# Handing 29 of the first 64 ada weight chunks from VectorE to TensorE in a two-block fp32 transformer kernel

## The chip, the cores and the metric

One NeuronCore of one Trainium2 chip runs the whole program. The metric is the device time of one launch in microseconds (us), as the median of several runs. The kernel before takes 3055.92 us (3 runs, 3054.85 to 3061.74).

## The reference, cut to what matters

Two transformer blocks in fp32 on a sequence of 256 rows with model width 2048. The change touches only the very first step of the first block, the modulation vector, and what it feeds:

```python
mod = (c @ w_ada[l] + b_ada[l])[:, None, :]      # c: 1 x 2048, w_ada: 2048 x 12288
shift1, scale1, gate1, shift2, scale2, gate2 = jnp.split(mod, 6, axis=-1)
h = rmsnorm(x, g_pre_mix[l]) * (1.0 + scale1) + shift1
proj = h @ w_in[l]                               # everything else of the block follows from proj
```

`c @ w_ada` is one row times a matrix of 96 MB. Its first third (scale1 and shift1, 4096 columns, 32 MB) has to be known before `h`, and so before the first real matmul can run. The other two thirds are computed later, beside other work, and are not touched.

## The kernel before, in words

Everything is kept transposed: features on the 128 partitions, the 256 rows of the sequence along the free dimension.

**The matmul jobs.** All large matmuls go through one helper, `job` (its matmuls are recorded at line L1494). Weights arrive in chunks of 128 x 1024 fp32 in a ring of four `raw` slots. ScalarE rounds a chunk to `w_hi` (L607 for the first four chunks, L630 later), VectorE makes the rest `w_lo` (L967 for the first four, L1005 later), and TensorE multiplies both with the operand `X`. TensorE takes its instructions strictly in the order of its program, and the jobs follow each other from `kv`, the first, to the end of the kernel.

**The opening stage.** Before the job `kv` can go on, the kernel computes scale1 and shift1. The 32 MB are cut into 64 chunks, each of 128 rows of `w_ada` (index k, 16 of them) by 1024 columns (`ADA_CB`), 512 KB. Sixteen chunks make a block; the four blocks are taken in the order `FIRST_BLOCKS = (2, 0, 3, 1)`: scale1 first half, shift1 first half, scale1 second half, shift1 second half. So chunk number `at` is block `at // 16`, row group `at % 16`.

SyncE's queue loads the chunks in order into 12 staging slots (`stage`, L484), with x (`x1`, 2 MB) after chunk 5, the constants after chunk 9, and the first four `raw` chunks of `w_in` behind chunks 34 and 38 and at the end. Chunk n waits until VectorE has used chunk n - 12 (`stage_used`). A load that waits holds back all that stand behind it in the queue.

VectorE (`first_block`) multiplies each chunk by the 128 values of c that belong to its rows and adds it to an accumulator of 128 x 1024, `first_acc`: L1079 for the first chunk of a block, L1081 for the other 15. Between chunks it does other small work, put there by hand: results of the block before, the normalised x (`unit_x`, L1148), the bounds, the second half of X.

TensorE (`first_ada`) then adds the accumulator over the partitions: 8 matmuls, each with 128 columns of `first_acc` as the stationary operand and a 128 x 2 tile of ones as the moving one. The trace records each such fp32 matmul as two weight loads and two matmuls. VectorE adds the bias (`first_result`, L1089), and so on to the coefficients of X.

TensorE's own order in this stage is: `norm_sum(sq1)` (16 fp32 matmuls of 128 x 256 that add up the squares of x), `first_ada(0)`, `first_ada(1)`, `first_ada(2)`, then the first two chunks of the job `kv`, `first_ada(3)`, and the rest of `kv`. ScalarE squares x before `norm_sum` (L649) and makes the reciprocal root from its sum behind it (L652, L653). The first halves of X are written by ScalarE (L688) and the second ones by VectorE (L1113).

Of the kernel before, what the change touches and what calls it, by code (L numbers as in the profile page):

```python
# [16 lines left out]
P = 128  # L17
# [22 lines left out]
ADA_CB = 1024  # L40
STAGES = 12
FIRST_BLOCKS = (2, 0, 3, 1)

PAR = {}
# [98 lines left out]
def two_block_kernel(nc, xT, params, cons, level_in, count_in, hot_in, rel_bias, pos, w_ada, w_in, w_attn, w_hgrn, w_out,  # L144
                     w_ffn_in, w_ffn_out, w_in2, pool_w, w_out2, w_up, w_down, out, stop_after=None):
    ctx = ExitStack()
    with ctx:
# [117 lines left out]
        def sem(name):  # L265
            return ctx.enter_context(nc.semaphore(name))
# [10 lines left out]
        ada_pair, ada_half, ada_split = sem("ada_pair"), sem("ada_half"), sem("ada_split")  # L277
        ada_mm, ada_out = sem("ada_mm"), sem("ada_out")
        staged = [sem(f"staged{n}") for n in range(STAGES)]
        stage_used, mod_ready = sem("stage_used"), sem("mod_ready")  # L280
        dve_chain = sem("dve_chain")
        act_chain = sem("act_chain")
        act_parted, sp_parted, pool_parted = sem("act_parted"), sem("sp_parted"), sem("pool_parted")
# [71 lines left out]
        def ahead(j, i, p, final):  # L355

            q = p + RING
            if q < j.n:
                return j, i, q
            if not final:  # L360
                return j, i + 1, q - j.n
            return (j.next, 0, q - j.n) if j.next is not None else None

        def half_slot(j, q):

# [98 lines left out]
        def P_(name, a=0, b=None):  # L464
            lo, hi = PAR[name]
            return par[:, lo + a:(hi if b is None else lo + b)]
# [6 lines left out]
        @block.sync  # L473
        def _(sp):
            sp.dma_start(par[:, :], params).then_inc(par_in, 16)
            ada_v = w_ada.rearrange("(k p) n -> p k n", p=P)

            def first_weights(q):
                sp.dma_start(raw[:, q, :, :], w_src(jobs[0], 0, q)).then_inc(landed[q], 16)
            for n in range(ADA_FIRST * DT):  # L480
                m, k, s = FIRST_BLOCKS[n // DT], n % DT, n % STAGES
                if n >= STAGES:
                    sp.wait_ge(stage_used, n - STAGES + 1)
                sp.dma_start(stage[s][:, :], ada_v[:, k, m * ADA_CB:(m + 1) * ADA_CB]).then_inc(staged[s], 16)  # L484
                if n == 5:
                    sp.dma_start(x1[:, :, :], xT.rearrange("(t p) s -> p t s", p=P)).then_inc(x_in, 16)
                if n == 9:
                    sp.dma_start(con[:, :], cons).then_inc(con_in, 16)
                if live and n in (2 * DT + 2, 2 * DT + 6):
                    first_weights(0 if n == 2 * DT + 2 else 1)  # L490
            for q in (2, 3) if live else ():
                first_weights(q)

            def load(j, i, k, src, flat_=False):

                s = slot_of(j, k)
                sp.wait_ge(raw_used, landing(j, i, k) - RING + 1)
                if not is_static(i):
                    sp.sem_inc(sp_parted, 1)
                dst = raw[:, s, :, :].rearrange("p k n -> p (k n)") if flat_ else raw[:, s, :, :]  # L500
                sp.dma_start(dst, src).then_inc(landed[s], 16)

            def job_turn(j, i, final):
                for p in range(j.n):
                    nxt = ahead(j, i, p, final)
                    if nxt:
                        load(j, i, j.at[p], w_src(*nxt))
                    for k, a in enumerate(j.ada):
                        if a == p:
                            load(j, i, j.ada_at(k), ada_v[:, k, ds((j.m0 + i) * ADA_CB, ADA_CB)], True)  # L510
            for j in live:
                all_turns(sp, j, job_turn)
# [435 lines left out]
        def _(dve):  # L948
# [119 lines left out]
            def first_block(n, between={}):  # L1068
                for k in range(DT):
                    at = n * DT + k  # L1070
                    s = at % STAGES
                    if k == 0 and n >= 2:
                        dve.wait_ge(ada_mm, n - 1)
                    if k >= 1:
                        dve.wait_ge(stage_used, at)
                    dve.wait_ge(staged[s], 16 * (at // STAGES + 1))
                    ck, acc = P_("c", k, k + 1), first_acc[:, n % 2, :]
                    if k == 0:
                        ins = nc.vector.tensor_scalar(acc, stage[s][:, :], ck, None, ALU.mult)  # L1079
                    else:  # L1080
                        ins = nc.vector.scalar_tensor_tensor(acc, stage[s][:, :], ck, acc, ALU.mult, ALU.add)  # L1081
                    ins.then_inc(stage_used, 1)
                    if k in between:
                        between[k]()

            def first_result(n):
                m = FIRST_BLOCKS[n]
                dve.wait_ge(ada_mm, n + 1)
                nc.vector.tensor_tensor(mod[:, m * 8:m * 8 + 8], pss[:, 3, 496:512:2], P_("b_ada", m * 8, m * 8 + 8), ALU.add  # L1089
                                        ).then_inc(ada_out, 1)  # L1090

            def first_scale(n):
                first_result(n)
                dve.wait_ge(ada_out, n + 1)
                t0 = 8 * (n // 2)
                here(nc.vector.scalar_tensor_tensor(coef[:, 0, t0:t0 + 8], mod[:, DT + t0:DT + t0 + 8], 1.0,
                                                    P_("g_pre_mix", t0, t0 + 8), ALU.add, ALU.mult))

            def first_shift(n):
                first_result(n)  # L1100
                dve.wait_ge(ada_out, n + 1)
                dve.sem_inc(mod_ready, 1)

            def first_full(q):
                for t in range(4 * q, 4 * q + 4):
                    ins = nc.vector.tensor_scalar(sq1[:, t, :], x1[:, t, :], coef[:, 0, t:t + 1], mod[:, t:t + 1],
                                                  ALU.mult, ALU.add)
                here(ins)

            def first_low(q):  # L1110
                t = slice(4 * q, 4 * q + 4)
                dve.wait_ge(nrm_hi, q + 1)
                nc.vector.tensor_tensor(X[:, t, S:2 * S], sq1[:, t, :], X[:, t, 0:S].bitcast(F32), ALU.subtract  # L1113
                                        ).then_inc(nrm_out, 1)
# [35 lines left out]
            def bounds():  # L1150
# [6 lines left out]
                here(nc.vector.tensor_scalar(cosq[:, :], cosk[:, :], HD1 ** -0.5, None, ALU.mult))  # L1157
                here(nc.vector.tensor_scalar(sinq[:, :], sink_[:, :], HD1 ** -0.5, None, ALU.mult))

            first_block(1, {4: lambda: first_scale(0), 6: unit_x, 10: bounds})  # L1160
            splits = (lambda: split_first(0), lambda: split_first(1)) if live else (lambda: None,) * 2
            first_block(2, {4: lambda: first_shift(1), 6: lambda: first_full(0), 7: lambda: first_low(0),
                            9: lambda: first_full(1), 10: lambda: first_low(1), 12: splits[0], 14: splits[1]})
            first_block(3, {4: lambda: first_scale(2)})
            if live:
                split_first(2)
# [325 lines left out]
        def _(pe):  # L1492
            def mm(out_, l, r_, start=True, stop=True):
                return nc.tensor.matmul(out_, l, r_, start=start, stop=stop)  # L1494
# [76 lines left out]
                        pe.wait_ge(nrm_out, 4 * k + c + 1)  # L1571
                return ready

            norm_sum(sq1)

            def first_ada(n):
                pe.wait_ge(stage_used, (n + 1) * DT)
                if n:
                    pe.wait_ge(ada_out, n)
                for t in range(8):  # L1580
                    ins = mm(pss[:, 3, 496 + 2 * t:498 + 2 * t], first_acc[:, n % 2, t * P:(t + 1) * P], ones[:, 0:2])
                ins.then_inc(ada_mm, 1)
            pe.wait_ge(ones_set, 2)
            for n in range(3):
                first_ada(n)
            pe.sem_inc(S1["pv"], 1)
            pe.sem_inc(SH["sb"], 1)
            pe.sem_inc(SH["o"], 1)
            if runs("kv"):
                pe.wait_ge(con_in, 16)  # L1590
                pe.wait_ge(ones_set, 3)

                def side(i, p):
                    if p == 1:
                        first_ada(3)
                job(J["kv"], lambda g: X, x_ready(), side)

                def side(i, p):
                    if is_first(i):
                        return  # L1600
                    if p == 0:

                        mm(pss[:, 0, 0:S], C_("rope_swap"), proj[:, KA, :]).then_inc(S1["swap"], 1)
                        for a in range(2):
                            ins = nc.tensor.transpose(pss[:, 2, a * P:(a + 1) * P], proj[:, VA, a * P:(a + 1) * P], C_("ident"))
                        ins.then_inc(S1["vt"], 1)
                    if p == 2:

                        pe.wait_ge(S1["kr"], 1)
                        for g in range(2):  # L1610
                            mm(pss[:, 1, g * S:(g + 1) * S], C_("kv_pick", g * P, (g + 1) * P), kr[:, :]).then_inc(S1["dup"], 1)
                job(J["qa"], lambda g: X, None, side)
# [235 lines left out]
```

## Time and profile before

| | |
|---|---|
| median of 3 runs | 3055.92 us |
| the profiled execution | 3053.75 us |
| its span | 3052.0 us |
| mean granted TensorE clock | 0.925 |
| TensorE matmul busy | 2674.7 us, 88% |
| VectorE busy | 1833.3 us, 60% |
| ScalarE busy | 1310.0 us, 43% |
| DMA | 550.85 MB, mean 180 GB/s |

Busy times are those of one profiled execution, and shares are shares of its span. The profiled execution is 2.17 us under the median of the runs. A granted clock of 1.00 is 2.4 GHz, 0.50 is 1.2 GHz. Rows are in us from the start of the span unless they say ns; "x16" is a count of recorded instructions, and what stands behind "<-" in a row of a tile is what is read. PEld is TensorE's weight load, PE its matmul, SPq SyncE's DMA queue, DVE VectorE, ACT ScalarE.

### The profile page before, as it was taken

Reading aid. Unit: us, or ns where it says so; the run is one execution under the profiler, and the core shown is the slowest. Engines: PE = TensorE matmul, PEld = TensorE weight load, DVE = VectorE, ACT = ScalarE, POOL = GpSimd, SP = SyncE. Lnnn points to the kernel's source line nnn. Section 1 sums busy time; section 2 is a strip of 40 time slices with the busy share of each in tenths; the row PEclk is TensorE's granted clock in tenths of the full one; section 3 lists DMA queues with packets and bytes.
Section 4 is the critical chain, followed back from the end, with each engine's and each line's share of the span. In section 5 each row is a group of like instructions: output and inputs, shape, how many; then the busy total and the mean of one; then the engine's idle time right before and its main releaser. Section 6 shows DMA issues by size and latency. Waiting matters only on the chain.

```text
span 3052.0 us, 40694 instructions
## 1 busy us (share of the span) xinstructions
PE 2674.7 (88%) x14562; PEld 2302.2 (75%) x14562; DVE 1833.3 (60%) x2057; ACT 1310.0 (43%) x1585; POOL 73.4 (2%) x56
## 2 busy tenths in 40 slices
PE   2598886666799769999979999799889999999998
PEld 1577776565687658888768887688778888888887
DVE  7766665666566655556655554644547766456664
ACT  1244443333443344444334444454445555445542
POOL 0000000000000000000000000001000000000000
PEclk7798887878899879999989999899899999999999
DMA  9767773222368726668756655365344566555664
GB/s 379 229 198 228 239 234 105 86 78 83 103 188 274 250 80 186 186 185 261 257 185 182 187 188 166 102 180 154 110 145 154 177 191 193 189 179 184 192 190 141
DMA packets 473580, 550.85 MB, mean 180 GB/s; under 512 B 16728, under 2 KB 446816, under 8 KB 473488
## 3 DMA queue, kind: packets, MB, share of 16 engines
q1 hardware_dynamic: 471408, 542.10, 56.0%
q0 software_dynamic: 2080, 7.52, 0.8%
q8 instruction: 59, 0.97, 0.1%
q14 instruction: 33, 0.27, 0.0%
HBM read 547.44 MB, written 2.11 MB: 180 GB/s over the span
## 4 chain that ended last, share of the span: by engine, by line
PE 66%; DVE 12%; issue 10%; DMA 5%; ACT 5%; POOL 1%; SPq 1%; ACTq 0%; DVEq 0%; POOLq 0%
PE psg L1494 60%; PE pss L1494 5%; ACT w_hi L630 2%; DMA raw<-in_w_ffn_out 2%; DVE first_acc L1081 2%; DMA raw<-in_w_out 2%; DVE w_lo L1005 2%; DVE s_ab L1298 1%; DVE ada_acc L986 1%; DVE masked L1295 1%; POOL ada_acc L529 1%; DMA raw<-in_w_ffn_in 1%; DVE Pq L1281 1%; DVE sq L1042 0%; DVE X L1047 0%
## 5 line engine op out<-in xcount | busy, mean ns | idle before, releaser
L1494 PE MATMUL psg<-X,w_hi 128*128 128x512 f32 x4768 | 1721.0, 406 | 35.2 <-issue 22.1
L1005 DVE TENSOR_TENSOR w_lo<-raw,w_hi 128x1024 fp32r<-128x1024 f32 x832 | 1024.7, 1244 | 914.3 <-ACT w_hi L630 905.7
L1494 PE MATMUL psg<-X,w_lo 128*128 128x256 f32 x4768 | 1331.4, 284 | 0.0
L630 ACT ACTIVATE w_hi<-raw 128x1024 fp32r<-128x1024 f32 x832 | 869.2, 1056 | 1055.8 <-PE psg L1494 851.0
L1494 PEld LDWEIGHTS psg<-X,w_hi 128*128 128x128 f32 x4768 | 908.6, 192 | 253.4 <-issue 28.2
L1494 PEld LDWEIGHTS psg<-X,w_lo 128*128 128x128 f32 x4768 | 921.4, 193 | 14.6 <-issue 1.7
L1494 PE MATMUL psg<-hid,w_hi 128*128 128x512 f32 x1408 | 494.2, 395 | 2.2 <-DVE w_lo L1005 2.1
L1494 PE MATMUL psg<-hid,w_lo 128*128 128x256 f32 x1408 | 388.5, 280 | 0.0
L1494 PEld LDWEIGHTS psg<-hid,w_hi 128*128 128x128 f32 x1408 | 262.7, 188 | 63.8 <-DVE w_lo L1005 3.4
L1494 PEld LDWEIGHTS psg<-hid,w_lo 128*128 128x128 f32 x1408 | 264.8, 188 | 2.9
L986 DVE SCALAR_TENSOR_TENSOR ada_acc<-raw,par,ada_acc 128x1024 f32<-128x1024 f32 x112 | 142.7, 1280 | 5.1 <-DMA raw<-in_w_ada 4.9
L614 ACT ACTIVATE half<-psg 128x512 f32<-128x512 f32 x205 | 119.2, 581 | 10.1 <-PE psg L1494 10.1
L1464 DVE SCALAR_TENSOR_TENSOR cacc<-cu,par,cacc 128x256 f32<-128x256 f32 x176 | 81.5, 483 | 49.4 <-ACT cacc L851 43.2
L1494 PE MATMUL psg<-merged,w_hi 128*128 128x512 f32 x256 | 95.3, 413 | 6.1 <-DVE w_lo L1005 6.1
L1494 PE MATMUL pss<-Pq,Rk 128*128 128x128 f32 x224 | 43.4, 371 | 48.3 <-DVE r_c L1289 48.3
L1081 DVE SCALAR_TENSOR_TENSOR first_acc<-stage,par,first_acc 128x1024 f32<-128x1024 f32 x60 | 77.1, 1285 | 12.6 <-DMA stage<-in_w_ada 10.5
L1494 PE MATMUL pss<-sq,ones 128*128 128x256 f32 (+1 forms) x144 | 46.8, 493 | 42.0 <-ACT sq L649 41.8
L1494 PEld LDWEIGHTS pss<-Pq,Rk 128*128 128x128 f32 x224 | 41.3, 283 | 50.7 <-issue 50.7
L851 ACT ACTIVATE cacc<-cu,par 128x256 f32<-128x256 f32 x88 | 48.2, 595 | 71.5 <-DVE cu L974 71.5
L1494 PEld LDWEIGHTS pss<-sq,ones 128*128 128x128 f32 x144 | 34.1, 242 | 53.7 <-issue 45.8
L1494 PE MATMUL psg<-merged,w_lo 128*128 128x256 f32 x256 | 72.2, 287 | 0.0
L1494 PE MATMUL pss<-ones,first_acc 128*128 128x2 f32 x64 | 14.3, 353 | 65.7 <-DVE first_acc L1081 65.7
(275 smaller groups left out, 1641.1 us busy)
## 6 DMA issues: line engine op xcount, KB each, us to landing
raw<-in_w_in SPq DMA_DIRECT2D x212, 512.0 KB, 3.9
raw<-in_w_ffn_in SPq DMA_DIRECT2D x176, 512.0 KB, 3.6
raw<-in_w_up SPq DMA_DIRECT2D x176, 512.0 KB, 4.7
raw<-in_w_ada SPq DMA_DIRECT2D x128, 512.0 KB, 4.8
raw<-in_w_ffn_out SPq DMA_DIRECT2D x88, 512.0 KB, 4.5
raw<-in_w_down SPq DMA_DIRECT2D x88, 512.0 KB, 4.4
stage<-in_w_ada SPq DMA_DIRECT2D x64, 512.0 KB, 8.7
raw<-in_w_out SPq DMA_DIRECT2D x64, 512.0 KB, 3.7
```

What stands on the lines that cost most here:

```text
L529: nc.gpsimd.tensor_tensor(acc[:, 0, :], acc[:, 0, :], acc[:, 1, :], ALU.add).then_inc(ada_pair, 1)
L614: nc.scalar.activation(half[:, b // 2, :, :], psg[:, b:b + 2, CW:2 * CW], ACT.Copy).then_inc(half_ready, 1)
L630: nc.scalar.activation(w_hi[:, half_slot(j, p), :, :], raw[:, slot_of(j, k), :, :], ACT.Copy).then_inc(hi_ready, 1)
L851: nc.scalar.activation(cacc[:, g, a, :], cu[:, g, a, 2:], ACT.Identity, scale=par[:, ds(2 * i + o, 1)], bias=par[:, ds(2 * i + ob, 1)]).th ...
L986: nc.vector.scalar_tensor_tensor(acc[:, k % 2, :], w, ck, acc[:, k % 2, :], ALU.mult, ALU.add).then_inc(raw_used, 1)
L1005: nc.vector.tensor_tensor(w_lo[:, hs, :, :], raw[:, slot_of(j, j.at[p]), :, :], w_hi[:, hs, :, :].bitcast(F32), ALU.subtract).then_inc(raw ...
L1081: ins = nc.vector.scalar_tensor_tensor(acc, stage[s][:, :], ck, acc, ALU.mult, ALU.add)
L1281: nc.vector.tensor_tensor(Pq[:, :, :], decay[:, 0:7, :], mid(hg_q[:, :], 7), ALU.mult)
L1295: step(nc.vector.tensor_tensor(masked[:, :, :].rearrange("p l s -> p (l s)"), pss[:, 2 * a:2 * a + 2, :].rearrange("p t s -> p (t s)"), le ...
L1298: nc.vector.tensor_reduce(s_ab[:, a, :], masked[:, :, :].rearrange("p l s -> p s l"), AX.X, ALU.add).then_inc(SH[m_], 1)
L1464: ins = nc.vector.scalar_tensor_tensor(cacc[:, g, a, :], cu[:, g, a, tap_:tap_ + CW], par[:, ds(2 * i + o, 1)], cacc[:, g, a, :], ALU.mult ...
L1494: return nc.tensor.matmul(out_, l, r_, start=start, stop=stop)
```

## The change

29 of the 64 chunks (`FIRST_PE`) are no longer multiplied and added by VectorE. TensorE takes them straight from their staging slot: eight matmuls for a chunk, each with 128 columns of the slot as the stationary fp32 operand and two neighbouring columns of c as the moving one (only the first of the two results is used). They are the chunks with odd k, without k = 15 in blocks 0 to 2: seven in each of the first three blocks, eight in the last. The other 35 (`FIRST_DVE`) stay with VectorE: nine in each of the first three blocks, eight in the last. Each TensorE chunk leaves its eight results in columns of its own in `pss`, the accumulator's sum leaves eight more, and `first_result` adds them up with one more VectorE instruction, a `tensor_reduce`, before it adds the bias.

A slot of a TensorE chunk is freed by TensorE (`stage_summed`), one of a VectorE chunk by VectorE. TensorE's order becomes: terms and sum of block 0, `norm_sum(sq1)`, terms and sum of blocks 1 and 2, the first four terms of block 3, the first two chunks of `kv`, three more terms of block 3, its sum, its last term, the rest of `kv`. VectorE's small pieces of work between chunks move to chunks that it still has (`unit_x` from k = 6 to k = 8, the bounds from k = 10 to k = 12, and those of block 2 likewise).

```diff
--- before.py
+++ after.py
@@ -40,6 +40,8 @@
 ADA_CB = 1024
 STAGES = 12
 FIRST_BLOCKS = (2, 0, 3, 1)
+FIRST_PE = tuple(n * 16 + k for n in range(4) for k in range(16) if k % 2 and (k < 15 or n == 3))
+FIRST_DVE = tuple(n for n in range(64) if n not in FIRST_PE)
 
 
 PAR = {}
@@ -277,7 +279,7 @@
         ada_pair, ada_half, ada_split = sem("ada_pair"), sem("ada_half"), sem("ada_split")
         ada_mm, ada_out = sem("ada_mm"), sem("ada_out")
         staged = [sem(f"staged{n}") for n in range(STAGES)]
-        stage_used, mod_ready = sem("stage_used"), sem("mod_ready")
+        stage_used, stage_summed, mod_ready = sem("stage_used"), sem("stage_summed"), sem("mod_ready")
         dve_chain = sem("dve_chain")
         act_chain = sem("act_chain")
         act_parted, sp_parted, pool_parted = sem("act_parted"), sem("sp_parted"), sem("pool_parted")
@@ -361,6 +363,9 @@
                 return j, i + 1, q - j.n
             return (j.next, 0, q - j.n) if j.next is not None else None
 
+        def first_terms(n):
+            return 1 + sum(at // DT == n for at in FIRST_PE)
+
         def half_slot(j, q):
 
             return (j.h0 + q) % RING
@@ -479,8 +484,11 @@
                 sp.dma_start(raw[:, q, :, :], w_src(jobs[0], 0, q)).then_inc(landed[q], 16)
             for n in range(ADA_FIRST * DT):
                 m, k, s = FIRST_BLOCKS[n // DT], n % DT, n % STAGES
-                if n >= STAGES:
-                    sp.wait_ge(stage_used, n - STAGES + 1)
+                before = n - STAGES
+                if before in FIRST_DVE:
+                    sp.wait_ge(stage_used, FIRST_DVE.index(before) + 1)
+                if before in FIRST_PE:
+                    sp.wait_ge(stage_summed, FIRST_PE.index(before) + 1)
                 sp.dma_start(stage[s][:, :], ada_v[:, k, m * ADA_CB:(m + 1) * ADA_CB]).then_inc(staged[s], 16)
                 if n == 5:
                     sp.dma_start(x1[:, :, :], xT.rearrange("(t p) s -> p t s", p=P)).then_inc(x_in, 16)
@@ -1069,10 +1077,12 @@
                 for k in range(DT):
                     at = n * DT + k
                     s = at % STAGES
+                    if at not in FIRST_DVE:
+                        continue
                     if k == 0 and n >= 2:
                         dve.wait_ge(ada_mm, n - 1)
                     if k >= 1:
-                        dve.wait_ge(stage_used, at)
+                        dve.wait_ge(stage_used, FIRST_DVE.index(at))
                     dve.wait_ge(staged[s], 16 * (at // STAGES + 1))
                     ck, acc = P_("c", k, k + 1), first_acc[:, n % 2, :]
                     if k == 0:
@@ -1086,7 +1096,10 @@
             def first_result(n):
                 m = FIRST_BLOCKS[n]
                 dve.wait_ge(ada_mm, n + 1)
-                nc.vector.tensor_tensor(mod[:, m * 8:m * 8 + 8], pss[:, 3, 496:512:2], P_("b_ada", m * 8, m * 8 + 8), ALU.add
+                dve.wait_ge(stage_summed, sum(at < (n + 1) * DT for at in FIRST_PE))
+                terms = pss[:, 2 + n % 2, 0:16 * first_terms(n)].rearrange("p (j t z) -> p t j z", t=8, z=2)[:, :, :, 0]
+                here(nc.vector.tensor_reduce(coef[:, 2, 0:8], terms, AX.X, ALU.add))
+                nc.vector.tensor_tensor(mod[:, m * 8:m * 8 + 8], coef[:, 2, 0:8], P_("b_ada", m * 8, m * 8 + 8), ALU.add
                                         ).then_inc(ada_out, 1)
 
             def first_scale(n):
@@ -1157,10 +1170,10 @@
                 here(nc.vector.tensor_scalar(cosq[:, :], cosk[:, :], HD1 ** -0.5, None, ALU.mult))
                 here(nc.vector.tensor_scalar(sinq[:, :], sink_[:, :], HD1 ** -0.5, None, ALU.mult))
 
-            first_block(1, {4: lambda: first_scale(0), 6: unit_x, 10: bounds})
+            first_block(1, {4: lambda: first_scale(0), 8: unit_x, 12: bounds})
             splits = (lambda: split_first(0), lambda: split_first(1)) if live else (lambda: None,) * 2
-            first_block(2, {4: lambda: first_shift(1), 6: lambda: first_full(0), 7: lambda: first_low(0),
-                            9: lambda: first_full(1), 10: lambda: first_low(1), 12: splits[0], 14: splits[1]})
+            first_block(2, {4: lambda: first_shift(1), 6: lambda: first_full(0), 8: lambda: first_low(0),
+                            10: lambda: first_full(1), 12: lambda: first_low(1), 14: splits[0], 15: splits[1]})
             first_block(3, {4: lambda: first_scale(2)})
             if live:
                 split_first(2)
@@ -1571,18 +1584,39 @@
                         pe.wait_ge(nrm_out, 4 * k + c + 1)
                 return ready
 
+            def first_terms_of(n, ats):
+                for at in ats:
+                    pe.wait_ge(staged[at % STAGES], 16 * (at // STAGES + 1))
+                    j = FIRST_PE.index(at) - sum(b // DT < n for b in FIRST_PE)
+                    c2 = par[:, PAR["c"][0] + at % DT:PAR["c"][0] + at % DT + 2]
+                    for t in range(8):
+                        o = 16 * j + 2 * t
+                        ins = mm(pss[:, 2 + n % 2, o:o + 2], stage[at % STAGES][:, t * P:(t + 1) * P], c2)
+                    ins.then_inc(stage_summed, 1)
+
+            def first_sum(n):
+                pe.wait_ge(stage_used, sum(at < (n + 1) * DT for at in FIRST_DVE))
+                for t in range(8):
+                    o = 16 * (first_terms(n) - 1) + 2 * t
+                    ins = mm(pss[:, 2 + n % 2, o:o + 2], first_acc[:, n % 2, t * P:(t + 1) * P], ones[:, 0:2])
+                return ins
+
+            def first_own(n):
+                return [at for at in FIRST_PE if at // DT == n]
+
+            def first_ada(n):
+                if n >= 2:
+                    pe.wait_ge(ada_out, n - 1)
+                first_terms_of(n, first_own(n))
+                first_sum(n).then_inc(ada_mm, 1)
+            pe.wait_ge(par_in, 16)
+            pe.wait_ge(ones_set, 2)
+            first_ada(0)
             norm_sum(sq1)
-
-            def first_ada(n):
-                pe.wait_ge(stage_used, (n + 1) * DT)
-                if n:
-                    pe.wait_ge(ada_out, n)
-                for t in range(8):
-                    ins = mm(pss[:, 3, 496 + 2 * t:498 + 2 * t], first_acc[:, n % 2, t * P:(t + 1) * P], ones[:, 0:2])
-                ins.then_inc(ada_mm, 1)
-            pe.wait_ge(ones_set, 2)
-            for n in range(3):
+            for n in (1, 2):
                 first_ada(n)
+            pe.wait_ge(ada_out, 2)
+            first_terms_of(3, first_own(3)[:4])
             pe.sem_inc(S1["pv"], 1)
             pe.sem_inc(SH["sb"], 1)
             pe.sem_inc(SH["o"], 1)
@@ -1592,7 +1626,9 @@
 
                 def side(i, p):
                     if p == 1:
-                        first_ada(3)
+                        first_terms_of(3, first_own(3)[4:7])
+                        first_sum(3).then_inc(ada_mm, 1)
+                        first_terms_of(3, first_own(3)[7:])
                 job(J["kv"], lambda g: X, x_ready(), side)
 
                 def side(i, p):
```

## Rows read from the trace of the kernel before

**Rows 1.** Stretches of the opening: length, busy time (instructions) by engine, granted clock, DMA share, GB/s.

```profile
40.00:60.00 20.00, 0.36 (x2) 0.28 (x2) 19.40 (x21) 0.72 (x2) 0.00 (x0) 0.50 1.03 405
60.00:80.00 20.00, 3.58 (x16) 3.49 (x16) 19.21 (x26) 6.16 (x10) 0.00 (x0) 0.50 1.03 405
...
100.00:120.00 20.00, 10.23 (x47) 9.05 (x46) 17.13 (x16) 1.06 (x1) 0.00 (x0) 0.67 0.63 209
120.00:140.00 20.00, 16.25 (x85) 14.07 (x85) 14.11 (x19) 12.00 (x17) 0.65 (x1) 0.83 0.64 196
```

**Rows 2.** The chain that ended last, where the opening ends: start, us, what.

```profile
116.51 3.59 PE pss L1494 x16
...
120.89 1.58 ACT X L688 x3
122.56 1.23 DVE X L1113
123.83 32.62 PE psg L1494 x176
```

**Rows 3.** Waits of SyncE's queue, first 150 us: total, times, longest.

```profile
SPq L484 <- DVE first_acc L1081: 53.3, 43, 5.4
```

**Rows 4.** The tile first_acc: ns min/median/max, first and last start, forms.

```profile
L1494 PE MATMUL pss<-ones,first_acc x64: 345/353/375, 36.8 to 119.7; 128*128 128x2 f32 x64
L1081 DVE SCALAR_TENSOR_TENSOR first_acc<-stage,par,first_acc x60: 1278/1285/1286, 9.6 to 115.2; 128x1024 f32<-128x1024 f32 x60
```

**Rows 5.** Timeline of all engines, 0 to 50 us: start, us, what [idle before].

```profile
9.62 6.57 DVE L1081 SCALAR_TENSOR_TENSOR first_acc<-stage,par,first_acc 128x1024 f32<-128x1024 f32 x5 [3.19 <-DMA stage<-in_w_ada]
...
22.08 5.25 DVE L1081 SCALAR_TENSOR_TENSOR first_acc<-stage,par,first_acc 128x1024 f32<-128x1024 f32 x4 [5.89 <-DMA stage<-in_w_ada]
...
23.28 9.42 PE L1494 MATMUL pss<-sq,ones 128*128 128x256 f32 x32 [23.28 <-ACT sq L649]
...
34.52 0.42 ACT L653 ACTIVATE rstd<-lnv 128x256 f32<-128x256 f32 x1
...
36.82 3.55 PE L1494 MATMUL pss<-ones,first_acc 128*128 128x2 f32 x16 [4.12 <-DVE first_acc L1081]
...
47.16 0.16 DVE L1089 TENSOR_TENSOR mod<-pss,par 128x8 f32<-128x8 f32 x1
```

**Rows 6.** Timeline of TensorE from the third accumulator sum into the job kv.

```profile
95.75 3.57 PE L1494 MATMUL pss<-ones,first_acc 128*128 128x2 f32 x16 [23.80 <-DVE first_acc L1081]
99.19 0.77 PE L1494 MATMUL psg<-X,w_hi 128*128 128x512 f32 x1
...
106.46 0.28 PE L1494 MATMUL psg<-X,w_lo 128*128 128x256 f32 x1
```

**Rows 7.** Timeline of TensorE at a later sum of two columns, inside a job.

```profile
257.40 1.94 PE L1494 MATMUL pss<-ones_r,ada_hl 128*128 128x2 f32 x16 [0.68 <-POOL ada_hl L534]
259.20 0.48 PE L1494 MATMUL psg<-X,w_hi 128*128 128x512 f32 x1
```

**Rows 8.** Short stretches where the granted clock changes, same columns as rows 1.

```profile
26.00:28.00 2.00, 2.00 (x7) 1.59 (x5) 1.29 (x2) 1.27 (x1) 0.00 (x0) 1.00 1.01 405
28.00:30.00 2.00, 2.00 (x11) 1.77 (x10) 1.22 (x1) 0.00 (x0) 0.00 (x0) 1.00 1.05 418
...
34.60:34.80 0.20, 0.00 (x0) 0.00 (x0) 0.20 (x1) 0.20 (x1) 0.00 (x0) 0.79 1.07 430
...
101.00:102.00 1.00, 1.00 (x5) 0.86 (x4) 0.93 (x4) 0.00 (x0) 0.00 (x0) 0.50 0.77 258
...
103.00:104.00 1.00, 1.00 (x7) 0.90 (x6) 0.96 (x2) 0.00 (x0) 0.00 (x0) 1.00 0.99 373
...
109.80:110.00 0.20, 0.00 (x0) 0.00 (x0) 0.16 (x2) 0.01 (x1) 0.00 (x0) 0.53 1.09 348
...
259.40:260.00 0.60, 0.60 (x5) 0.52 (x5) 0.60 (x2) 0.00 (x0) 0.00 (x0) 1.00 0.79 136
260.00:261.00 1.00, 1.00 (x5) 0.83 (x4) 0.84 (x3) 0.00 (x0) 0.00 (x0) 0.50 0.85 311
```

## The prediction, made before the changed kernel was timed

> **What bounds the kernel now.** I read the table of stretches first, because the change touches only the opening. From 40 to 80 us VectorE is busy for 19.4 and 19.2 of every 20 us, DMA moves 405 GB/s at a share of 1.03, and TensorE does next to nothing at a granted clock of 0.50 [rows 1]. So two things run at their limit there: the loads, and VectorE, which needs 1.285 us for a chunk [rows 4], about what 512 KB take at 405 GB/s (1.29 us). The queue's own waits show which is the tighter: it waited 43 times, 53.3 us in all, for VectorE to free a slot [rows 3]. The chain of work that ended last says where the opening ends: the last accumulator sum starts at 116.51, ScalarE and VectorE finish X, and the job `kv` resumes at 123.83 and then runs on for 32.6 us without a gap [rows 2]. TensorE's program is one line from there to the end, and it has no prefetch deeper than four chunks that could absorb a shift. So the whole change is worth what it does to one number, the 123.83 us at which `kv` resumes. If VectorE alone set it, taking 29 x 1.285 = 37 us off VectorE would help until the loads are the limit.
>
> **The change part by part.** What is new is work on TensorE: 29 chunks of 8 matmuls with a 128 x 128 fp32 stationary operand and two moving columns. The trace has this very form, from `first_acc` instead of from a slot, with 16 records of each kind for 8 matmuls [rows 4]. Its price depends on the clock, and the rows show both:
>
> - At 0.50 such a group, begun at 95.75, lets the next matmul start at 99.19, so 3.44 us for a group in a stream [rows 6]; alone it lasts 3.55 to 3.57 [rows 5, 6].
> - At 1.00 a group of 16 records (fp32r, also two moving columns), begun at 257.40, lets the next start at 259.20, so 1.80 us [rows 7].
>
> Chunks for TensorE come in one out of two, so every 2 x 1.29 = 2.6 us. At 1.80 us TensorE keeps up. At 3.44 us it does not and is the new bound of the opening. So the question that decides is the clock during a long stream of such matmuls.
>
> Rows speak for the slow clock. The group from 95.75 to 99.2 keeps TensorE busy without a gap and runs straight into `kv`, and still the clock is 0.50 at 101 to 102 us and is 1.00 only from 103 on, 3.8 us after the first wide matmul [rows 6, 8]. And a group takes the clock away: TensorE goes from 257.40 through the two-column group into wide matmuls with no gap, and at 260.0 the granted clock falls from 1.00 to 0.50 while it is fully busy [rows 7, 8]. [...] I take 3.44 us for the stream, and 1.80 only for what is left of a full clock after wide work.
>
> The Trainium skill speaks the other way here. Its page "TensorE: Matmul & The Clock Gate", in the closing table "Why this matters for your kernels", says to keep TensorE busy continuously to get to the full clock, and its section "LDWEIGHTS (loading the stationary operand)" prices a load at its columns divided by 1.2 GHz. An estimate by that page is 16 x 107 ns = 1.7 us for a group, half of what the row at the slow clock shows; by it TensorE would keep up, which is the first rival below. Against it stands the row of 3.44 us, and the fall at 260.0.
>
> Now TensorE's line, in its new order, in us from the start:
>
> 1. Chunks 1, 3 and 5 are there early (VectorE takes the first five behind chunk 0 from 9.62 on without a gap) and are done by 9.6 + 3 x 3.44 = 19.9. Chunk 6 lands at 22.08, behind x, and chunk 7 is there by 23.4, when VectorE takes it [rows 5]. Then 4 terms and the sum: 23.4 + 5 x 3.44 = 40.6. In the kernel before the same sum is done at 40.4 [rows 5], so block 0 gains nothing.
> 2. `norm_sum`, which stood ahead of this at 23.28, is now behind it. It begins at the slow clock, as it did before (7 records in the 2 us from 26, 11 in the 2 us from 28 [rows 8]; the clock printed ahead of the first change is not to be read), so 9.4 us again [rows 5]: 50.0. Behind it on TensorE wait the terms of block 1. Behind its result waits VectorE's `unit_x`, at k = 8 of block 1, until about 52.2 (rstd ended 2.2 us after it [rows 5]), while VectorE could be there at 45. That stall costs nothing: after `unit_x` (5 us) it has four more chunks and the bounds, and is done near 64, and TensorE asks for the sum of block 1 only near 72.
> 3. Blocks 1 and 2: 14 terms and 2 sums, 16 x 3.44 = 55.0. From this goes what runs at the clock that `norm_sum` leaves. In the trace the clock falls some 2.1 us after it [rows 5, 8]. Each us at full clock saves 3.44 / 1.80 - 1 = 0.91 us, so 1.9. Result 103.1.
> 4. Four terms of block 3: 13.8, to 116.9. The slots follow: chunk 63 waits for TensorE's second term of this block and is issued near 110.
> 5. Two chunks of `kv`: 99.19 to 106.74, 7.55 us, with the same slow start [rows 6]: 124.4. Before, this was hidden while VectorE worked; now it lies on the path.
> 6. Three terms, the sum, the last term: 5 x 3.44 = 17.2, less 0.91 x 3.2 = 2.9 for the clock that `kv` leaves (it ends at 106.7 and the clock falls at 109.8 [rows 6, 8]), plus 0.1 until the last result is written: 138.8.
> 7. To the resumption of `kv`: from 120.08 to 123.83 before, 3.75 us [rows 2], plus the `tensor_reduce` over 8 x 9 numbers. The nearest row is the 128 x 8 addition at 0.16 us [rows 5]; between that and 0.5 I take 0.25. That gives 142.8.
>
> VectorE's and the queue's parts are costed at nothing, because TensorE's line hides them: VectorE's chunks of a block and the small work between them are done some 8 us before TensorE reaches the sum, in blocks 1 and 2 alike, and VectorE then waits for TensorE's slots. The queue, in order, now waits for `stage_summed`, and each load that waits holds the VectorE chunk behind it; this is why VectorE's speed buys nothing. If that cover were gone (a fast TensorE), VectorE's share would be 38 us shorter and the loads would be next.
>
> The sum is 142.8 - 123.83 = 19.0 us later. Against the profiled execution: 3053.75 + 19.0 = 3072.8. The median of the runs is 2.2 us above that execution, so 3055.92 + 19.0 = 3075.
>
> **Bounds.** Low: chunk 7 at 22.1 (-1.3), and the clock staying up 1.5 us longer after each of the two wide pieces (-2.7): 15 us. High: no leftover of the clock at all (+4.8), every group as long as a lone one, 0.13 x 34 (+4.4), `norm_sum` slow to its end, which at 7 records in 2 us costs near 3 more: 31 us. The likeliest case's own range is 3069 to 3083.
>
> **The rivals.**
>
> - *TensorE's clock rises in the stream, or most of it* (the other side). Price: 1.80 us a group. Then block 0 is bound by its loads: chunk 13 lands near 31.5, so its sum is near 35, `norm_sum` ends near 43, and blocks 1 and 2 wait for loads. All 64 chunks, x, the constants, the parameters and two `raw` chunks are 37.5 MB, at 405 GB/s 93 us, so chunk 63 lands near 96; the last term ends near 98, `kv` resumes near 102, 22 us earlier: 3034. It decides if a group costs under 2.6 us. For it: the page above, and VectorE at 97% [rows 1]. Against it: rows 7 and 8. Chance 0.08.
> - *The clock comes and goes*: wide work and the stream mix so that the mean group costs about 2.85 us, 34 x 0.6 = 20 us less than in my sum, and it comes out even: 3056. For it: `norm_sum` and the two chunks of `kv` do raise the clock. Against it: that is only some 5 us of 117. Chance 0.03.
> - *More than my sum*: each chunk's wait for its slot, and then for the next load, drains TensorE, so that lockstep between SyncE, VectorE and TensorE adds to it. At 1 us for each of the 29 chunks it would be 3104. Against it: at 3.44 us a group every TensorE chunk has landed some 15 us before its turn. Chance 0.05.
>
> **How the numbers follow.** My case has 0.84. The range 3065 to 3086 takes in the bounds on either side and the near part of the last rival, and leaves out the first two. 0.2% is 6 us and is about what the runs can tell apart. Slower by more than that: 0.84 + 0.05 = 0.89; within it 0.03; faster 0.08.
>
> **What would show it.** In the changed profile: a granted clock of 0.50 from 25 us to near 120 except behind `norm_sum`; TensorE weight loads from `stage` at 333 ns, 16 records in 3.4 us, back to back; VectorE's waits for TensorE or for a load, DMA far under 405 GB/s from 50 us on; `kv` resuming near 143. I am wrong if the terms run at 1.00, or the groups overlap so that one costs under 2.6 us; then the loads bound the opening and the kernel is faster.

## The result and the profile after

The changed kernel takes 3076.38 us (median of 5 runs, 3071.8 to 3078.11) against 3054.85 (5 runs, 3052.62 to 3061.74): a ratio of 1.0061, 95% interval 1.0047 to 1.0074, which is 14.4 to 22.6 us slower. Its profiled execution took 3071.8 us with a span of 3070.0, 18.0 us over the span before; it is the fastest of its five runs, and the two medians are 21.5 us apart. The prediction was 3075 in 3065 to 3086.

First the table of stretches of the changed kernel, for the same four stretches as [rows 1] and the one between them, 80 to 100 us.

```profile
40.00:60.00 20.00, 20.00 (x109) 18.54 (x108) 15.45 (x20) 4.28 (x7) 0.00 (x0) 0.89 0.85 318
60.00:80.00 20.00, 20.00 (x96) 20.00 (x95) 14.47 (x25) 6.04 (x10) 0.00 (x0) 0.50 1.03 398
80.00:100.00 20.00, 20.00 (x96) 20.00 (x95) 11.15 (x12) 0.00 (x0) 0.00 (x0) 0.50 0.93 319
100.00:120.00 20.00, 20.00 (x92) 19.09 (x93) 7.98 (x8) 1.06 (x1) 0.00 (x0) 0.57 0.82 273
120.00:140.00 20.00, 15.91 (x88) 15.58 (x87) 4.27 (x9) 4.67 (x9) 0.65 (x1) 0.60 0.08 26
```

The row of the kernel before that [rows 1] leaves out:

```profile
80.00:100.00 20.00, 4.25 (x19) 4.15 (x20) 19.75 (x20) 0.00 (x0) 0.00 (x0) 0.50 0.86 278
```

The reader should see the columns trade places. VectorE, busy for 17 to 20 of every 20 us before and for 14 from 120 us, is down to 8 to 15 and, from 120 us, 4. TensorE is busy for every one of the 20 us up to 120 us, with as many weight loads as matmuls, and from 60 to 100 us its granted clock is 0.50 in spite of that. The loads come later than before: from 40 to 60 us they move 318 GB/s where it was 405, from 60 to 80 us 398, and what is missing is made up behind, 319 and 273 GB/s where it was 278 and 209.

The chain that ended last in the changed kernel, up to 160 us, to be held against [rows 2]:

```profile
37.50 75.86 PE pss L1507 x368
113.36 7.42 PE psg L1507 x32
120.78 13.93 PE pss L1507 x80
...
134.81 0.24 DVE coef L1101
...
135.84 1.58 ACT X L696 x3
...
137.51 1.24 DVE X L1126
...
138.79 21.31 PE psg L1507 x105
```

From 37.5 to 134.7 us it never leaves TensorE. L1507 is the matmul helper (L1494 before). The job `kv` resumes at 138.79 instead of 123.83, 15.0 us later. SyncE's queue, which had waited for VectorE [rows 3], now waits for TensorE, and so does VectorE itself (two views of the changed kernel, waits of the queue and of all engines in the first 150 us):

```profile
SPq L492 <- PE pss L1507: 57.7, 21, 8.9
```

```profile
DVE coef L1101 <- PE pss L1507: 29.4, 3, 19.4
DVE first_acc L1091 <- DMA stage<-in_w_ada: 27.4, 13, 7.3
```

TensorE's timeline in the changed kernel shows each step of the predicted line:

```profile
23.12 13.81 PE L1507 MATMUL pss<-par,stage 128*128 128x2 f32 x64 [3.29 <-DMA stage<-in_w_ada]
37.50 3.58 PE L1507 MATMUL pss<-ones,first_acc 128*128 128x2 f32 x16 [0.57 <-DVE first_acc L1091]
40.93 9.35 PE L1507 MATMUL pss<-sq,ones 128*128 128x256 f32 x32
...
50.12 18.87 PE L1507 MATMUL pss<-par,stage 128*128 128x2 f32 x112
68.85 3.55 PE L1507 MATMUL pss<-ones,first_acc 128*128 128x2 f32 x16
72.26 24.03 PE L1507 MATMUL pss<-par,stage 128*128 128x2 f32 x112
96.15 3.55 PE L1507 MATMUL pss<-ones,first_acc 128*128 128x2 f32 x16
99.57 13.79 PE L1507 MATMUL pss<-par,stage 128*128 128x2 f32 x64
```

Seven terms in 96.15 - 72.26 = 23.9 us are 3.41 us a term. The same seven in block 1 take only 68.85 - 50.12 = 18.7 us. Short stretches of the changed kernel say why:

```profile
54.00:55.00 1.00, 1.00 (x11) 1.00 (x10) 1.00 (x1) 0.66 (x2) 0.00 (x0) 1.00 1.00 393
55.00:56.00 1.00, 1.00 (x9) 1.00 (x9) 0.97 (x2) 0.00 (x0) 0.00 (x0) 0.81 1.00 406
56.00:57.00 1.00, 1.00 (x6) 1.00 (x6) 0.96 (x2) 0.00 (x0) 0.00 (x0) 0.50 1.06 381
```

The clock that `norm_sum` leaves lasts until 55.6, and at that clock there are 11 records in a us instead of 6 or 7. TensorE is busy without a break when the clock falls.

### The profile page after: what moved, and what is told of

Its sections match the earlier page's. It is cut to its first block, busy times and chain, and to the rows that moved or that the text cites. A ratio compares the mean times of both kernels' runs of the same rounds, so it can differ in the third digit from the quotient of the medians.

```text
span 3070.0 us, 41571 instructions
## 1 busy us (share of the span) xinstructions
PE 2764.2 (90%) x15026; PEld 2392.1 (78%) x15026; DVE 1799.2 (59%) x2032; ACT 1309.6 (43%) x1585; POOL 73.4 (2%) x56
## 4 chain that ended last, share of the span: by engine, by line
PE 69%; issue 10%; DVE 10%; DMA 6%; ACT 5%; POOL 1%; ACTq 0%; DVEq 0%; SPq 0%; POOLq 0%
PE psg L1507 60%; PE pss L1507 8%; ACT w_hi L638 2%; DMA raw<-in_w_ffn_out 2%; DMA raw<-in_w_out 2%; DVE w_lo L1013 1%; DVE ada_acc L994 1%; DVE s_ab L1311 1%; DMA stage<-in_w_ada 1%; DVE masked L1308 1%; POOL ada_acc L537 1%; DMA raw<-in_w_ffn_in 1%; DVE Pq L1294 1%; DVE sq L1050 0%; DVE X L1055 0%
## 5 line engine op out<-in xcount | busy, mean ns | idle before, releaser
L1507 PE MATMUL psg<-X,w_hi 128*128 128x512 f32 x4768 | 1718.8, 406 | 36.4 <-issue 22.1
L1507 PE MATMUL psg<-X,w_lo 128*128 128x256 f32 x4768 | 1331.6, 284 | 0.0
L1507 PEld LDWEIGHTS psg<-X,w_hi 128*128 128x128 f32 x4768 | 907.8, 192 | 253.7 <-issue 28.4
L1507 PEld LDWEIGHTS psg<-X,w_lo 128*128 128x128 f32 x4768 | 921.2, 193 | 14.7 <-issue 1.7
L1507 PE MATMUL psg<-hid,w_hi 128*128 128x512 f32 x1408 | 494.6, 395 | 1.2 <-DVE w_lo L1013 1.2
L1507 PE MATMUL psg<-hid,w_lo 128*128 128x256 f32 x1408 | 389.2, 280 | 0.0
L1507 PEld LDWEIGHTS psg<-hid,w_hi 128*128 128x128 f32 x1408 | 263.1, 188 | 62.4 <-DVE w_lo L1013 2.1
L1507 PEld LDWEIGHTS psg<-hid,w_lo 128*128 128x128 f32 x1408 | 265.3, 188 | 2.9
L1507 PE MATMUL pss<-par,stage 128*128 128x2 f32 x464 | 91.7, 335 | 12.7 <-DMA stage<-in_w_ada 12.7
L1507 PEld LDWEIGHTS pss<-par,stage 128*128 128x128 f32 x464 | 91.6, 309 | 12.9 <-issue 9.4
L1507 PE MATMUL psg<-merged,w_hi 128*128 128x512 f32 x256 | 94.5, 410 | 7.9 <-DVE w_lo L1013 7.9
L1507 PE MATMUL pss<-Pq,Rk 128*128 128x128 f32 x224 | 41.3, 359 | 48.3 <-DVE r_c L1302 48.3
L1507 PEld LDWEIGHTS pss<-Pq,Rk 128*128 128x128 f32 x224 | 39.3, 271 | 50.6 <-issue 50.6
L1507 PE MATMUL pss<-ones_r,ada_hl 128*128 128x2 f32 x128 | 24.9, 324 | 55.8 <-POOL ada_hl L542 55.8
L1507 PE MATMUL psg<-merged,w_lo 128*128 128x256 f32 x256 | 71.6, 285 | 0.0
L1507 PEld LDWEIGHTS pss<-ones_r,ada_hl 128*128 128x128 f32 x128 | 24.2, 291 | 58.4 <-POOL ada_hl L542 54.7
```

## The experiments

Rivals: the fp32 loads or the hand-over of slots in lockstep are slow whatever the clock; the new place of `norm_sum` is what costs; `kv`'s two chunks are hidden. The measure is the time at which `kv` resumes, read in each kernel's chain; the medians have the rest of the kernel in them as well. "Before" is always the kernel before, run beside the variant.

**128 columns instead of 2.** Both operands are otherwise the same; of each result only the first column is kept. The one k = 15 chunk stays narrow.

```diff
-                    c2 = par[:, PAR["c"][0] + at % DT:PAR["c"][0] + at % DT + 2]
+                    cols = 128 if at % DT < DT - 1 else 2
+                    c2 = par[:, PAR["c"][0] + at % DT:PAR["c"][0] + at % DT + cols]
...
-                        ins = mm(pss[:, 2 + n % 2, o:o + 2], stage[at % STAGES][:, t * P:(t + 1) * P], c2)
+                        ins = mm(pss[:, 2 + n % 2, o:o + cols], stage[at % STAGES][:, t * P:(t + 1) * P], c2)
```

> 28 of the 29 TensorE chunks stream 128 moving columns instead of 2 (only the first column of each result is kept; the next matmul overwrites the rest); everything else is the changed kernel. Clock theory (narrow moving operands do not count as activity, so the clock stays at 0.50 and a group costs 3.44 us): the granted clock goes to 1.00 within the first groups and stays, the group costs 1.8 to 1.9 us, the opening is then bound by its loads (chunk 63 lands near 101 to 107) and the job kv resumes at 107 to 114 us instead of 138.8, so 25 to 32 us faster than the changed kernel and some 10 to 15 us faster than the kernel before. Rival (the fp32 weight loads themselves are slow here, or slots handed over in lockstep bound the opening): 128 columns can only add work, kv resumes at 138 us or later and the clock or the group cost does not move.

Measured: 3051.5 us, 0.9975 of before (0.9963 to 0.9987). `kv` resumes at 113.94, 24.9 us earlier than with 2 columns, although 64 times as many columns are streamed. Its stretches and pieces of its timeline:

```profile
40.00:60.00 20.00, 20.00 (x141) 18.70 (x139) 17.43 (x25) 4.28 (x7) 0.00 (x0) 0.94 0.99 374
60.00:80.00 20.00, 17.02 (x129) 16.29 (x128) 15.58 (x22) 6.05 (x10) 0.00 (x0) 0.91 1.03 404
```

```profile
47.34 12.67 PE L1507 MATMUL pss<-par,stage 128*128 128x128 f32 x112
...
72.92 2.05 PE L1507 MATMUL pss<-par,stage 128*128 128x128 f32 x16 [0.51 <-DMA stage<-in_w_ada]
75.46 2.05 PE L1507 MATMUL pss<-par,stage 128*128 128x128 f32 x16 [0.49 <-DMA stage<-in_w_ada]
```

From 60 to 80 us the clock is 0.91 on average, a lone group takes 2.05 us with its tail, and TensorE now waits for loads, which are back at 404 GB/s. Seven groups in a stream at full clock, from 47.34, take 12.67 us or 1.81 each, what the two-column group of [rows 7] costs (1.80). Where the clock does fall in this run, its groups are as slow as the narrow ones:

```profile
64.00:65.00 1.00, 1.00 (x7) 1.00 (x6) 0.00 (x0) 0.00 (x0) 0.00 (x0) 0.50 1.04 414
67.00:68.00 1.00, 1.00 (x11) 1.00 (x10) 0.36 (x1) 0.00 (x0) 0.00 (x0) 1.00 1.06 385
```

That is 7 records in a us at 0.50 and 11 at 1.00, as with two columns. This is the run that settles the cause: only the moving width differs, and a group costs what the clock gives it at either width. It also rejects the idea that the weight loads are slow by themselves. Two things that I expected did not come: the clock did not stay up (0.84 from 20 to 40 us, 0.83 from 80 to 100), and the kernel is 4.8 us under the one before by the medians, not 10 to 15.

**Half of the matmuls.** Four matmuls of four columns per TensorE chunk; half of those products are left out. All hand-overs stay.

```diff
-                    c2 = par[:, PAR["c"][0] + at % DT:PAR["c"][0] + at % DT + 2]
-                    for t in range(8):
+                    c2 = par[:, PAR["c"][0] + at % DT:PAR["c"][0] + at % DT + 4]
+                    for t in range(0, 8, 2):
```

> Each TensorE chunk gets 4 matmuls of 4 moving columns instead of 8 of 2; half of its products are left out. The number of chunks, of slot hand-overs and of waits is that of the changed kernel. Theory that TensorE's own time per group is the bound: a group costs 1.72 us at the slow clock (which stays 0.50), the 29 groups save up to 50 us of TensorE, the loads bound the opening and kv resumes at 107 to 114 us. Rival (lockstep between SyncE's queue, the slots and TensorE costs a fixed time per hand-over): resumption stays above 130 us.

Measured: 3045.16 us, 0.9962 of before (0.9946 to 0.9977); `kv` resumes at 112.91. From its timeline and its stretches:

```profile
75.67 1.87 PE L1507 MATMUL pss<-par,stage 128*128 128x4 f32 x8 [0.69 <-DMA stage<-in_w_ada]
```

```profile
60.00:80.00 20.00, 14.92 (x69) 14.75 (x69) 16.25 (x22) 6.04 (x10) 0.00 (x0) 0.50 1.04 404
```

The clock is 0.50 as in the changed kernel, the number of waits is the same, and 26 us are gone. So the bound was TensorE's time per group, not the number of hand-overs.

**16 chunks instead of 29.**

```diff
-FIRST_PE = tuple(n * 16 + k for n in range(4) for k in range(16) if k % 2 and (k < 15 or n == 3))
+FIRST_PE = tuple(n * 16 + k for n in range(4) for k in (1, 5, 9, 13))
```

> Only 16 chunks go to TensorE (k = 1, 5, 9, 13 of each block), 48 stay with VectorE; same code otherwise. Theory of a TensorE bound at 3.44 us a group: TensorE's line loses 13 groups, 45 us, and is no longer the bound; VectorE ends its chunks near 101 (80 us of work after 36 less 12 x 1.31), the loads near 101 to 107 because norm_sum still holds back the slots of TensorE chunks from 40 to 50 us; kv resumes at 107 to 113 us, 11 to 17 us before the 123.8 of the kernel before: 3038 to 3046 us. Rival (taking chunks to TensorE at all costs time, by the reduction, the order of norm_sum or contention): kv resumes at or after 123.8 us and the time is not under the kernel before.

Measured: 3051.38 us, 0.9984 of before (0.9974 to 0.9995), which is under 1 but not clearly by the 0.2% set as the limit, and over the 3038 to 3046 us expected. `kv` resumes at 117.36, 6.5 us ahead of before, but 4 us later than the end of the expected range. Its chain and its timeline show where the rest went:

```profile
103.71 7.97 PE psg L1507 x32
...
117.36 33.29 PE psg L1507 x176
```

```profile
111.53 1.84 PE L1507 MATMUL pss<-ones,first_acc 128*128 128x2 f32 x16
```

VectorE had its last chunk done at 104.1 us, but the sum had to wait for the first two chunks of `kv`, which start at 103.71 and come first in TensorE's program. I had left this out of the expectation. The rival that any chunk on TensorE is a loss falls.

**norm_sum ahead of everything again**, as in the kernel before, with 29 chunks.

```diff
-            first_ada(0)
             norm_sum(sq1)
+            first_ada(0)
```

> norm_sum(sq1) goes back ahead of the first block on TensorE, 29 chunks otherwise as in the changed kernel. Theory (TensorE's program is one line): TensorE idles to 23.3, norm_sum ends at 32.7, and the three groups that ran from 9.5 to 19.8 now stand behind it, so the end of the line moves by about 7 to 10 us: kv resumes at 145 to 149. Rival (moving norm_sum behind the first block is what costs, through the late rstd and the slots held for 9 us): kv resumes before 138 us.

Measured: 3080.69 us, 1.0086 of before (1.0065 to 1.0108); `kv` resumes at 148.08, 9.3 us later than in the changed kernel, as the serial line has it. Behind `norm_sum` seven terms again take less than at 3.44 us each, 19.4 us for 24.1. Its timeline:

```profile
23.06 8.75 PE L1507 MATMUL pss<-sq,ones 128*128 128x256 f32 x32 [23.06 <-ACT sq L657]
31.65 19.41 PE L1507 MATMUL pss<-par,stage 128*128 128x2 f32 x112
```

**norm_sum behind the third term.**

```diff
-            first_ada(0)
+            first_terms_of(0, first_own(0)[:3])
             norm_sum(sq1)
+            first_terms_of(0, first_own(0)[3:])
+            first_sum(0).then_inc(ada_mm, 1)
```

> The changed kernel (29 chunks, 2 columns) with norm_sum placed behind the third term of block 0, in the gap from 19.8 to 23.1 us in which TensorE waits for the load behind x. Theory of one serial TensorE line: 3.3 us of idle time go, and the clock that norm_sum leaves is spent on the terms of block 0 instead of block 1, so kv resumes 3 to 5 us earlier than 138.8, at 134 to 136. Rival (the late rstd and the slots held during norm_sum are the cost of its move): with norm_sum at about its old place, kv resumes 9 us or more earlier, at 130 or before.

Measured: 3073.52 us, 1.0075 of before (1.005 to 1.0099); `kv` resumes at 137.85, only 0.9 us earlier. Its timeline:

```profile
9.24 10.37 PE L1507 MATMUL pss<-par,stage 128*128 128x2 f32 x48 [9.24 <-DMA stage<-in_w_ada]
22.83 9.34 PE L1507 MATMUL pss<-sq,ones 128*128 128x256 f32 x32 [3.22 <-ACT sq L657]
32.01 8.63 PE L1507 MATMUL pss<-par,stage 128*128 128x2 f32 x64
```

My 3 to 5 us were wrong: the idle time before chunk 7 is also the time before the squares of x are ready (3.22 us idle, ended by ScalarE), so there was no gap to fill, and the leftover clock is spent once in either order (four terms in 8.6 us here). The rival is rejected all the same: with `norm_sum` at its old time and rstd early, the opening is within 1 us as late as in the changed kernel.

**Sum of block 3 ahead of kv.**

```diff
-            first_terms_of(3, first_own(3)[:4])
+            first_terms_of(3, first_own(3))
+            first_sum(3).then_inc(ada_mm, 1)
...
-                def side(i, p):
-                    if p == 1:
-                        first_terms_of(3, first_own(3)[4:7])
-                        first_sum(3).then_inc(ada_mm, 1)
-                        first_terms_of(3, first_own(3)[7:])
-                job(J["kv"], lambda g: X, x_ready(), side)
+                job(J["kv"], lambda g: X, x_ready())
```

> The changed kernel with all eight terms of block 3 and its sum ahead of kv, so that kv is not interrupted. Theory (kv's first two chunks lie on TensorE's path as 7.4 us in front of the sum): the sum ends at 113.4 + 17.2 = 130.6, X is ready at about 134.9 while kv's first two chunks run to 138.1, so kv goes on from there without a gap and already at full clock, 3 to 5 us ahead of the changed kernel by its 16th chunk. Rival (kv's two chunks were hidden and the interruption costs nothing): no difference within 1 us.

Measured: 3069.37 us, 1.0057 of before (1.0038 to 1.0075). `kv` starts at 130.16 and is not interrupted (its chain); the first of ScalarE's `half` rows marks the end of its fourth chunk, here (second fence) and in the changed kernel (third, first 200 us alone):

```profile
130.16 34.94 PE psg L1507 x190
```

```profile
L622 ACT ACTIVATE half<-psg x205: 574/579/633, 143.9 to 3048.7; 128x512 f32<-128x512 f32 x103
```

```profile
L622 ACT ACTIVATE half<-psg x5: 577/578/622, 148.2 to 195.8; 128x512 f32<-128x512 f32 x5
```

143.9 against 148.2: 4.3 us. The fourth of these rows, behind the sixteenth chunk, starts at 181.5 here and at 185.8 in the changed kernel: 4.3 us again, within the 3 to 5 expected. `kv`'s two chunks did lie on the path, and the interruption had a price.

**20 chunks, and the order adjusted**, with 128 columns and with 2: five chunks a block (k = 1, 5, 9, 11, 13), `norm_sum` behind the second term, two terms of block 3 ahead of `kv` and three behind its second chunk. The first of the two has the `cols` edit above as well.

```diff
+FIRST_PE = tuple(n * 16 + k for n in range(4) for k in (1, 5, 9, 11, 13))
...
+            first_terms_of(0, first_own(0)[:2])
             norm_sum(sq1)
+            first_terms_of(0, first_own(0)[2:])
+            first_sum(0).then_inc(ada_mm, 1)
...
+            first_terms_of(3, first_own(3)[:2])
...
+                        first_terms_of(3, first_own(3)[2:])
                         first_sum(3).then_inc(ada_mm, 1)
```

> 20 chunks on TensorE (k = 1, 5, 9, 11, 13 of each block), 128 moving columns, norm_sum behind the second term of block 0, two terms of block 3 ahead of the first two chunks of kv and three behind. If TensorE's cold groups were the bound and nothing else, the loads now are: chunk 63 lands near 101, its last sum ends near 104, kv resumes at 107 to 110 us, the earliest so far, 3040 to 3046 us, under the kernel before and under the variant with 29 chunks and 128 columns. Rival (the loads still run late because slots of TensorE chunks come free late): kv resumes at 114 us or later.

> The same with 2 moving columns. Theory: the clock stays at 0.50, six groups of 3.44 us a block are 20.6 us, as long as the loads of a block take (16 x 1.29 = 20.7), so TensorE just keeps up and only the end differs: two terms to 90, kv's chunks to 98, three terms and the sum to 109, kv resumes at 111 to 115 us, 2 to 6 us behind the variant with 128 columns. Rival (with fewer chunks the columns no longer matter): both resume within 1 us of each other.

Measured: 3040.91 us with 128 columns, 0.9958 of before (0.9943 to 0.9973), and 3048.28 with 2, 0.9977 (0.9965 to 0.9989). `kv` resumes at 108.24 and 114.75, both within what was expected; they are 6.5 us apart where I had said 2 to 6. The stretch from 60 to 80 us, first with 128 columns, then with 2:

```profile
60.00:80.00 20.00, 15.08 (x96) 14.32 (x96) 18.86 (x25) 6.05 (x10) 0.00 (x0) 0.79 1.03 404
```

```profile
60.00:80.00 20.00, 18.27 (x85) 18.19 (x86) 19.07 (x25) 6.04 (x10) 0.00 (x0) 0.50 1.03 404
```

In both the loads run at their limit again. The 128-column version is the fastest kernel of the study that computes every product, 8 to 17 us under the kernel before by its interval.

## Why the prediction was right, and where it was not

- **That the opening decides, by the time at which `kv` resumes:** right. But the rest of the kernel does not stay put. From the resumption to the end of the span it is 2928.2 us before, 2931.2 in the changed kernel, and 2927.3 to 2933.2 in the seven variants whose resumption is read above from the chain. Of the 18.0 us between the two spans 15.0 are the opening; the other 3.0 lie behind it, inside this scatter, and I did not forecast them. By the medians the total is 21.5 us, which leaves 6.6 behind the opening; in the seven variants the shift of the median exceeds that of the resumption by -0.2 to 6.5 us. The predicted 19.0 came out near the measured total because my opening was 4 us too long and the rest at least 3 us longer than I said: the mechanism was right, but how near 3075 came to 3076.38 is luck. Of the 3.0 us, 1.2 can be read. The fourth chunk of `kv` ends 8.3 us after the resumption before (first fence) and 9.4 in the changed kernel (148.2, above), because the clock comes back later: over the first 11 us from the resumption it is 0.86 before (second fence) and 0.75 in the changed kernel (third). Why the rest is longer stays open.

```profile
132.10 0.58 ACT L614 ACTIVATE half<-psg 128x512 f32<-128x512 f32 x1
```

```profile
123.83:134.83 11.00, 10.99 (x55) 9.61 (x56) 8.84 (x11) 6.92 (x10) 0.00 (x0) 0.86 0.65 195
```

```profile
138.79:149.79 11.00, 11.00 (x48) 9.54 (x49) 8.54 (x11) 6.03 (x9) 0.00 (x0) 0.75 0.64 187
```

- **Steps 1 and 2**, block 0 and `norm_sum`: 40.6 and 50.0 predicted, 40.9 and 50.1 measured. `unit_x` starts at 52.5, with 52.2 predicted, after a stall of 3.6 us that cost nothing.
- **Step 3**, blocks 1 and 2: 3.44 us a group was right (3.41 to 3.42). The leftover of the clock was mis-sized: I took 2.1 us of full clock behind `norm_sum` from the trace before; it lasted 5.5 us, until 55.6, and saved 5.2 us instead of 1.9. In the two variants that move `norm_sum` it lasted 4.9 and 5.4 us. In the trace before TensorE was idle behind `norm_sum`, in these three it went on with narrow terms; whether that makes the difference was not tested. The step ended at 99.6, not 103.1. This one term makes up nearly the whole error of the opening.
- **Steps 4 to 6** (predicted, and measured in brackets): 13.8 us (13.8), `kv`'s two chunks 7.55 us (7.4), the last five groups 14.4 (13.9). That the two chunks come onto the path was shown by taking the interruption away.
- **Step 7**: 4.0 us predicted, 4.1 measured; the `tensor_reduce` is 0.24 us for my 0.25.
- **The bounds and the signs.** The high bound and the second rival count 34 groups; the steps add up to 33, which changes neither by more than 1 us. The weight loads at 333 ns and the waits of VectorE came as said. One sign did not: DMA was to be far under 405 GB/s from 50 us on, and from 60 to 80 us it moved 398.
- **The cause**, a clock that stays at 0.50 under two-column matmuls: shown by the run with 128 columns. Here the Trainium skill's page "TensorE: Matmul & The Clock Gate", in its closing table, ties the full clock to a TensorE that is kept busy; the trace after does not agree, with 0.50 from 56 us to past 113 while TensorE never pauses. The section "LDWEIGHTS (loading the stationary operand)" of that page of the Trainium skill, columns divided by 1.2 GHz, 107 ns for 128, does not say that the price follows the clock; the rows show 213 ns for a record at 0.50 and, in the group before at 1.00, 113.
- **Rivals**: of the faster one I had the sign and the condition right, but its time too low. With the clock up and 29 chunks `kv` resumed at 113.9, not 102, since chunk 63 did not land before about 100 in any version (the best one begins its last sum at 102.0) and the terms behind `kv`'s chunks still queue. Lockstep was rejected by halving the matmuls.

## What to carry to other kernels

Work moved to an idle engine has to be priced at the clock that this very work will get, not at that of the engine's busy stretches: here 37 us taken off VectorE became 29 x 3.44 = 100 us on TensorE, and the idle engine became the bound. When a narrow matmul is bound by its weight load, try a wider moving operand before giving up; the extra columns cost nothing here (1.81 us a group at full clock for 1.80) and the clock came up. And share work out by the slower engine's rate: of the three counts tried, 16, 20 and 29, 20 was the best, though the order of the pieces was changed with it.

## What the runs showed of the hardware that I had not expected

- Streaming more columns made the same work faster: groups of 16 loads with 128 columns took 2.05 us alone and 1.81 in a stream, at a clock of 1.00, and those with 2 columns 3.41 us in a stream at 0.50.
- The full clock that a wide piece of work leaves can last 2.1 us (before), 3.1 us (behind `kv`'s two chunks, in both kernels) or 4.9 to 5.5 us (behind `norm_sum` in the changed kernel and the two that move it) into narrow or idle time. A price taken from one such case carries an error of some 3 us.
- The part behind the opening, the same instructions in all these kernels, varied by 6 us of 2930 between profiled executions. A later start of the full clock in `kv` is 1.2 us of it in the changed kernel. The sum of slow stretches does not order the kernels: by the granted clock of the traces that part has 378 us at 0.50 before and 356 in the variant with 128 columns and 29 chunks, whose part is 5.0 us longer. The cause of the rest is not shown.
